# Gate projection by block products between the merge steps of the triangular inverse, with an image trip on two queues and another load order

## The chip, the core and the metric

The kernel runs on one core of one Trainium2 chip. The core has TensorE (PE, matrix products into PSUM), VectorE (DVE), ScalarE (ACT), GpSimd (POOL) and SyncE (SP, which here only issues DMAs), each with an instruction stream of its own; they wait for each other by semaphores. Sixteen DMA engines move data between HBM and SBUF. Everything is float32. The metric is the device time of one execution in microseconds (us), the median of the runs shown.

## The reference

One inference step of a decoder layer: 256 prompt tokens and 8 x 4 sample tokens, 288 columns in all, of width 1024. Cut to what matters here:

```python
h = rmsnorm(x, norm1_w)
proj = h @ w_in          # pool 512, q/k/v 3072, b/a 16, z 1024, gate_pool 1024, gate_delta 1024
...
A = (kb @ k.T) * decay * strict                  # per head and chunk of the sequence
t_inv = triangular_solve(eye + A, eye)           # unit lower triangular inverse
... # scan over chunks with t_inv; for samples: S = S * a + k_dec^T v_new
merged = sigmoid(gate_pool) * branch_pool + sigmoid(gate_delta) * branch_delta
x = x + merged @ w_out
x = x + moe(rmsnorm(x, norm2_w))                 # 32 experts, top 2; all experts' weights are read
```

The 16 column chunks of the two gates (128 columns each, 8 + 8) are the products that the change rewrites. The expert weights are 96 matrices of 1 MB.

## The kernel before

**Stages.** First the projection `proj = h @ w_in`, chunk by chunk of 128 output columns, with convolution, pooling and norms beside it; then the chunked delta rule: a prep per head, the inverse of `eye + A`, a scan; then the two branch products, the output product with the router, and eight quads of four experts each (gate, up, down). All engines follow orders written out by hand, one function per engine.

**Chunks and pairs.** A weight item of w_in is two chunks, 1 MB, in a ring slot of SBUF (`SLOT_OF` says which; slots 0 to 5). `proj(n)` (L1417) makes one chunk with eight products of 128x128 by 128x288, accumulated in PSUM bank n % 2; ScalarE evacuates it (`evac`, L951; tanh for the gates). Items 1 to 11 (`FAST`, the q/k/v chunks) are made another way: `fast_pair` (L1439) takes both chunks of an item as a 2 x 2 block matrix and makes seven block products (four products of 128x128 by 128x144 each) in place of eight. GpSimd forms four sums of weight blocks per pair (`sum_weights`, L754), VectorE had formed four sums of token blocks once, and VectorE and ScalarE add the products.

**Around the inverse.** The gate chunks are 36 to 51. The first nine (`LEAD_GATES`) run ahead of the inverse, the last seven (`LATE_GATES`) between its steps. The inverse needs the 16 x 16 diagonal blocks of A spread over partitions. This goes through DRAM: once all eight heads are prepared (`prep_done`), SP writes the image `a_image` (1 MB), reads eight blocks back (`diagonal_blocks`, L488), VectorE inverts them by forward substitution (15 steps, `sub_done`), SP writes eight blocks to `x_image` and reads it as X (256 KB). Then TensorE, VectorE and ScalarE merge the blocks 16 to 32, 32 to 64, 64 to 128: `inner_y`, `inner_xx`, `middle_y`, `middle_xx`, `outer_y`, `outer_xx` (L1688 to L1742).

**Sample states.** Between the merge steps stand four state units (`state_unit`, L1675: four products of 32x128 by 32x512). Each needs a spread of the new sample values over a tile `vx` (semaphore `vx_done`), and its results are added by VectorE (`state_adds`) to states that GpSimd has scaled after `sub_done`, eight operations of 128x1024 (L854). The first spread serves units 0 and 1, the second units 2 and 3; VectorE makes both (L2652).

**Loads.** SP issues everything in one order (a loop over the items, L560 on): each load waits until the reader of its slot is done. `DIAG_AT` puts the image trip into this order, `STORE_AT` the stores of the states. In the expert stage `gates`, `ups` and `downs` (L604 to L614) load four matrices each into fixed slots, once the products of an earlier quad have read them (`m_gate`, `m_up`, `m_dn1`); `pair_loads` (L647) sets their order.

Of the kernel before, what the change touches and what calls it, by code (L numbers as in the profile page):

```python
# [12 lines left out]
P = 128  # L13
# [8 lines left out]
H = 8  # L22
# [32 lines left out]
FAST = range(1, NQKV // 2)  # L55
SQUARES_AT = (2, 4, 7, 8)
HT, HK = T // 2, KD // 2
P1, P6, P5, P7, P2, P3, P4 = range(1, 8)
SUM2, SUM4, SUM7, SUM5, SUM6 = range(1, 6)
SLOT_OF = [i % 4 if i < NQKV // 2 else i % RA for i in range(A_ITEMS)]  # L60
# [6 lines left out]
def sums_slot(i):  # L67
    return 4 + i % 2


def reader_ahead(i, s):
    users = [j for j in range(i) if SLOT_OF[j] == s or (j in FAST and sums_slot(j) == s)]
    return max(users, default=None)
# [15 lines left out]
LEAD_GATES = 9  # L89
Z_AHEAD = 2  # L90
LATE_GATES = range(N_GATE + LEAD_GATES, N_PROJ)
# [10 lines left out]
STORE_AT = (IN_ITEMS + BP_ITEMS + 1, IN_ITEMS + BP_ITEMS + 3)  # L102
# [3 lines left out]
DIAG_AT = (N_GATE + 2) // 2 + RA - 1  # L106


EVEN_GATES, ODD_GATES = (8, 9, 11, 12), (2, 3, 4, 5)
UPS, DOWNS = (13, 14, 15, 6), (7, 10, 0, 1)  # L110
# [4 lines left out]
SECOND_DOWNS = (EARLY_DOWN,) + DOWNS[1:]  # L115

# [14 lines left out]
def hybrid_step(nc, x_prompt, x_sample, cache_pool, cache_conv, state_delta, norm1_w, w_in, w_pool,  # L131
# [24 lines left out]
    with ExitStack() as ctx:  # L156
# [250 lines left out]
        def item_read(i):  # L407
            if i < IN_ITEMS:
                return S["proj"], product(i, P4) if i in FAST else chunk(2 * i + 1)
# [10 lines left out]
        for n in range(N_PROJ):  # L420
            free[n] = (free[n - 1] if n else 0) + (1 if n // 2 in FAST else 2 if n < N_POOL else 3 if n < N_Z else 1)


        def chunk(n):
            return n + 1 + 5 * sum(1 for i in FAST if i < n // 2)
# [10 lines left out]
        def weights_summed(i, k):  # L436
            return 1 + 4 * FAST.index(i) + k
# [10 lines left out]
        def weight_sums(i):  # L448
            return slots[sums_slot(i)].rearrange("p (j k n) -> p j k n", j=4, k=HK)

# [12 lines left out]
        def delta_sums(j):  # L463
# [11 lines left out]
                      ((108, 109), o_norm_w)]  # L475
        block = ctx.enter_context(nc.Block())
# [3 lines left out]
        def _(sp):  # L480
# [7 lines left out]
            def diagonal_blocks():  # L488
                sp.wait_ge(S["prep_done"], H)
                sp.dma_start(a_image, AT.rearrange("p g i -> p (g i)")).then_inc(S["diag"], 16)  # L490
                sp.wait_ge(S["diag"], 16 * 2)
                for m in range(8):
                    sp.dma_start(And[16 * m:16 * m + 16, :].rearrange("g (j i) -> g j i", i=16),
                                 a_blocks[m].rearrange("j g i -> g j i")).then_inc(S["diag"], 16)
                sp.wait_ge(S["sub_done"], 1)
                for m in range(8):
# [2703 lines left out]
```

## Time and profile before

| | |
|---|---|
| median of 3 runs | 574.17 us (573.9 to 576.23) |
| profiled execution | 574.23 us, span 572.3 us |
| TensorE busy | 534.9 us, 93% of the span |
| VectorE, ScalarE, GpSimd busy | 280.1, 152.8, 138.1 us |
| chunk products (128x288) | 480 records, 122.6 us |
| block products (128x144) of the first stage | 616 records, 78.3 us |
| DMA queue of SP | 153.69 MB, 73.2% of 16 engines' span |

A float32 product stands twice in TensorE's records, so eight products of a chunk are 16 records. The span is the profiled part of the execution. Busy time is an average over stages with different limits; the stage table below tells them apart. A row of a timeline gives start, length, engine, line of the kernel, operation, tiles written and read, and count; in brackets the idle time ahead of it and what ended it.

### The profile page before, as it was taken

Reading aid. Unit: us, or ns where it says so; the run is one execution under the profiler, and the core shown is the slowest. Engines: PE = TensorE matmul, PEld = TensorE weight load, DVE = VectorE, ACT = ScalarE, POOL = GpSimd, SP = SyncE. Lnnn points to the kernel's source line nnn. Section 1 sums busy time; section 2 is a strip of 40 time slices with the busy share of each in tenths; the row PEclk is TensorE's granted clock in tenths of the full one; section 3 lists DMA queues with packets and bytes.
Section 4 is the critical chain, followed back from the end, with each engine's and each line's share of the span. In section 5 each row is a group of like instructions: output and inputs, shape, how many; then the busy total and the mean of one; then the engine's idle time right before and its main releaser. Section 6 shows DMA issues by size and latency. Waiting matters only on the chain. (4 is left out here: it accounts for less than half of the span.)

```text
span 572.3 us, 12784 instructions
## 1 busy us (share of the span) xinstructions
PE 534.9 (93%) x5156; PEld 405.9 (71%) x5156; DVE 280.1 (49%) x811; ACT 152.8 (27%) x408; POOL 138.1 (24%) x226
## 2 busy tenths in 40 slices
PE   7999999999999999999999999999998969599984
PEld 6899999877777776779799788657454535266442
DVE  3867768783543726446756344533523242405135
ACT  3258465315851002133100124210011101010105
POOL 6687677013030090024133222000000000000001
PEclk9999999999999999999999999999997989899988
DMA  9845454657984063853478898899999999999992
GB/s 259 239 124 155 122 161 149 213 174 268 319 253 148 10 219 106 254 155 108 128 259 341 350 424 299 347 396 425 401 421 420 419 420 423 420 419 420 419 361 96
DMA packets 81228, 158.00 MB, mean 276 GB/s; under 512 B 11166, under 2 KB 65067, under 8 KB 68979
## 3 DMA queue, kind: packets, MB, share of 16 engines
q1 hardware_dynamic: 78604, 153.69, 73.2%
q10 hardware_dynamic: 2567, 3.51, 2.1%
q8 instruction: 41, 0.67, 0.5%
q14 instruction: 16, 0.13, 0.1%
HBM read 149.40 MB, written 7.96 MB: 275 GB/s over the span
## 5 line engine op out<-in xcount | busy, mean ns | idle before, releaser
L1428 PE MATMUL ps<-arena 128*128 128x288 f32 x480 | 122.6, 410 | 1.7 <-issue 1.0
L1428 PEld LDWEIGHTS ps<-arena 128*128 128x128 f32 x480 | 89.4, 190 | 27.3 <-issue 3.1
L2092 PE MATMUL ps<-arena 128*32 128x256 f32 x1024 | 65.9, 417 | 15.0 <-DMA arena<-in_w_up_dram 13.4
L1435 PE MATMUL ps<-arena 128*128 128x144 f32 x616 | 78.3, 287 | 0.0
L1435 PEld LDWEIGHTS ps<-arena 128*128 128x128 f32 x616 | 76.3, 190 | 2.4 <-issue 1.9
L2092 PEld LDWEIGHTS ps<-arena 128*32 128x32 f32 x1024 | 38.0, 120 | 41.0 <-issue 25.6
L908 POOL TENSOR_TENSOR arena<-arena 128x512 f32<-128x512 f32 x2 | 2.5, 1276 | 207.2 <-ACT arena L1341 207.2
L2368 DVE SCALAR_TENSOR_TENSOR ps<-arena,ps 128x312 f32<-128x312 f32 x72 | 39.1, 545 | 2.2 <-ACT ps L1028 0.9
L1381 PE MATMUL ps<-arena 128*128 128x128 f32 (+7 forms) x162 | 26.7, 284 | 7.2 <-DVE arena L3069 5.1
L2007 PE MATMUL ps<-arena 128*128 128x128 f32 x256 | 32.3, 279 | 0.8 <-DVE arena L3047 0.7
L2007 PEld LDWEIGHTS ps<-arena 128*128 128x128 f32 x256 | 29.8, 192 | 3.7 <-issue 2.5
L1951 PE MATMUL ps<-arena 128*128 128x256 f32 x128 | 31.0, 385 | 0.0
L1381 PEld LDWEIGHTS ps<-arena 128*128 128x128 f32 (+7 forms) x162 | 18.9, 149 | 14.9 <-issue 6.4
L3069 DVE TENSOR_TENSOR arena<-arena,ps 128x256 f32<-128x256 f32 x8 | 3.4, 421 | 51.2 <-issue 40.8
L1903 PE MATMUL ps<-arena 128*128 128x144 f32 x224 | 27.9, 286 | 0.2 <-DVE arena L2887 0.2
L1903 PEld LDWEIGHTS ps<-arena 128*128 128x128 f32 x224 | 27.6, 190 | 0.6 <-DVE arena L2887 0.5
L2153 PE MATMUL ps<-arena 128*32 128x512 f32 x224 | 25.5, 595 | 0.6 <-ACT arena L1265 0.5
L3085 DVE TENSOR_TENSOR arena<-arena,ps 128x512 f32<-128x512 f32 (+1 forms) x35 | 21.6, 633 | 9.0 <-PE ps L2173 9.0
L1951 PEld LDWEIGHTS ps<-arena 128*128 128x128 f32 x128 | 23.1, 190 | 3.0 <-issue 0.4
L979 ACT ACTIVATE arena<-ps 128x288 f32<-128x288 f32 x16 | 6.6, 411 | 58.9 <-PE ps L1428 58.9
L3018 DVE COPY arena<-ps 128x512 f32<-128x512 f32 x8 | 5.5, 690 | 32.0 <-PE ps L2007 32.0
L3076 DVE COPY sc<-ps 128x512 f32<-128x512 f32 x7 | 4.8, 692 | 32.2 <-PE ps L2153 32.2
(442 smaller groups left out, 802.5 us busy)
## 6 DMA issues: line engine op xcount, KB each, us to landing
arena<-in_w_gate_dram SPq DMA_DIRECT2D x32, 1024.0 KB, 13.2
arena<-in_w_up_dram SPq DMA_DIRECT2D x32, 1024.0 KB, 16.9
arena<-in_w_down_dram SPq DMA_DIRECT2D x28, 1024.0 KB, 17.0
arena<-in_w_in_dram SPq DMA_DIRECT2D x26, 1024.0 KB, 5.8
out_dram<-arena SPq DMA_DIRECT2D x9, 512.0 KB, 7.2
arena<-in_w_branch_delta_dram SPq DMA_DIRECT2D x4, 1024.0 KB, 5.9
arena<-in_w_out_dram SPq DMA_DIRECT2D x4, 1024.0 KB, 5.2
arena<-in_state_delta_dram SPq DMA_DIRECT2D x7, 512.0 KB, 8.6
```

The costliest lines, as they stand in the source:

```text
L979: nc.scalar.activation(gT[:, n - N_GATE, :], src[:, 0:T], ACT.Tanh, scale=0.5).then_inc(S["proj_free"], 1)
L1381: return nc.tensor.transpose(out, in_, ident[0:m, 0:m])
L1428: last = mm(ps[n % 2][:, 0:T], w[:, k, P * (n % 2):P * (n % 2) + P], hT[:, k, :], start=(k == 0), stop=(k == KD - 1))
L1435: last = mm(to[:, 0:HT], left[:, k, :], right[:, k, :], start=(first and k == 0), stop=(k == HK - 1), skip_group_check=True)
L1903: last = mm(bank[:, 0:HT], left[:, k, :], right[:, k, :], start=(first and k == 0), stop=(k == HK - 1), skip_group_check=True)
L1951: last = mm(bank[:, 0:256], merged[:, k, P * t:P * t + P], w[:, k, :], start=(k == 0), stop=(k == KD - 1))
L2007: ins = mm(to, x2p[:, t, k, :], G[:, t, :], start=(first and k % 4 == 0), stop=(last_tile and k % 4 == 3), skip_group_check=True)
L2092: last = mm(to[CAP * e:CAP * e + CAP, 0:FE], xgT[:, k, CAP * e:CAP * e + CAP], w[e][:, k, :], start=(k == 0), stop=(k == KD - 1))
L2153: last = mm(ps[5 + half][CAP * e:CAP * e + CAP, :], actT[:, c, CAP * e:CAP * e + CAP], w[:, c, 512 * half:512 * half + 512], start=(c == 0 ...
L2368: ins = V.scalar_tensor_tensor(c, e[:, j:j + NACC], smallT[:, NQKV * j + n:NQKV * j + n + 1], c, ALU.mult, ALU.add)
L3018: V.tensor_copy(xgT[:, 0:4, :].rearrange("p k t -> p (k t)"), ps[0][:, :]).then_inc(S["m_xg0"], 1)
L3085: V.tensor_tensor(v, v, bank[:, 0:v.shape[1]], ALU.add).then_inc(S["m_yadd"], 1)
```

## The change

Three parts, in one diff.

1. Six early gate chunks stay before (36 to 41, `LEAD_GATES` = 6); the other ten become five pairs of seven block products (`LATE_FAST`, items 21 to 25). They use PSUM banks 0 and 1 alone, the sums of tokens are formed again into slot 0 and a spare strip (`sum_tokens`), and the sums of weights by GpSimd into slots 5 and 1 in turn. The first pair runs whole ahead of `inner_y`, the last whole behind the last state unit; the three between are cut into a piece of four blocks and a piece of three, laid between the merge steps. VectorE's additions and the merge steps are interleaved, a part of `middle_merge` goes to ScalarE, and the second spread (`vx`) goes to GpSimd.
2. The image trip: `a_image` is written in two parts (six heads, then two), and the eight block reads and eight block writes are split over SP's and ScalarE's queues.
3. Slots change (`SLOT_OF`, `ODD_GATES`, `DOWNS`); in the expert stage the third quad's up weights are loaded ahead of the second quad's down weights, and two of the third quad's down weights go to slots that the second quad's up weights leave (`third_downs`).

```diff
-LEAD_GATES = 9
+LEAD_GATES = 6
+LATE_FAST = range(IN_ITEMS - 5, IN_ITEMS)
+LEAD_PAIR, PAIR_A, PAIR_B, PAIR_C, PAIR_D = LATE_FAST
-DIAG_AT = (N_GATE + 2) // 2 + RA - 1
+DIAG_AT = LATE_FAST[1]
-STORE_AT = (IN_ITEMS + BP_ITEMS + 1, IN_ITEMS + BP_ITEMS + 3)
+STORE_AT = (IN_ITEMS + BP_ITEMS - 2, IN_ITEMS + BP_ITEMS - 1)
...
@@ SP @@
             def diagonal_blocks():
+                rows = AT.rearrange("p g i -> p (g i)")
-                sp.wait_ge(S["prep_done"], H)
-                sp.dma_start(a_image, AT.rearrange("p g i -> p (g i)")).then_inc(S["diag"], 16)
+                for heads, cols in ((IMAGE_FIRST // 2, slice(0, IMAGE_FIRST * P)), (H, slice(IMAGE_FIRST * P, 2 * H * P))):
+                    sp.wait_ge(S["prep_done"], heads)
+                    sp.dma_start(a_image[:, cols], rows[:, cols]).then_inc(S["diag"], 16)
...
                 if isinstance(i, int) and i == 0:
+                    ups(2, then)
                     downs(1, first + QE)
-                    ups(2, then)
                     gates(3, then + QE, 1)
+                    third_downs(then)
...
@@ GpSimd @@
             own_columns(1)
+            sum_weights(LATE_FAST[0])
             pool.wait_ge(S["sd_pe"], 2)
             nc.gpsimd.memset(X[:, 2 * H * TILE:6 * H * TILE], 0.0).then_inc(S["memsets"], 1)
             pool.wait_ge(S["sub_done"], 1)
+            sum_weights(LATE_FAST[1])
             for h in range(H):
                 nc.gpsimd.tensor_tensor(state[h], state[h], eGd[:, h, :].unsqueeze(2).to_broadcast([P, BD, P]),
                                         ALU.mult).then_inc(S["sd_mul"], 1)
+            sum_weights(LATE_FAST[2])
+            sum_weights(LATE_FAST[3])
+            pool.wait_ge(S["sdn_pe"], 2)
+            pool.wait_ge(S["decdve"], 8)
+            nc.gpsimd.tensor_tensor(vx, vnq[:, 1, :].unsqueeze(1).to_broadcast([P, BD, P]), spread(bmask4, P, P),
+                                    ALU.mult).then_inc(S["vx_done"], 1)
+            sum_weights(LATE_FAST[4])
...
@@ ScalarE @@
+            act.wait_ge(S["diag"], 16 * IMAGE_WRITES)
+            for m in BY_SCALAR:
+                read_diagonal(act, m)
             for n in range(N_GATE + 3, N_GATE + LEAD_GATES):
+                if n == N_GATE + LEAD_GATES - 1:
+                    act.wait_ge(S["sub_done"], 1)
+                    for m in BY_SCALAR:
+                        write_inverse(act, m)
                 evac(n)
...
@@ TensorE @@
+            def late_products(i):
...
+                late_block(0, a11, lambda k: hT[:, k, 0:HT])
+                pe.wait_ge(S["pads"], weights_summed(i, 2))
+                late_block(1, s2, lambda k: late_summed[1][k])
+                pe.wait_ge(S["proj_free"], late_free(i, 1))
+                late_block(0, s1, lambda k: late_summed[0][k])
+                pe.wait_ge(S["pads"], weights_summed(i, 3))
+                pe.wait_ge(S["sums"], late_added(i, L_SUM2))
+                late_block(1, s3, lambda k: late_summed[2][k])
+            def late_products_back(i):
...
+            late_products(LEAD_PAIR)
+            late_products_back(LEAD_PAIR)
             inner_y()
-            proj(LATE_GATES[0])
+            late_products(PAIR_A)
             inner_xx(0)
             state_unit(0)
             inner_xx(1)
-            proj(LATE_GATES[1])
+            late_products_back(PAIR_A)
             state_unit(1)
             middle_y()
-            proj(LATE_GATES[2])
+            late_products(PAIR_B)
             state_unit(2)
             middle_xx()
-            proj(LATE_GATES[3])
+            late_products_back(PAIR_B)
             outer_y()
-            proj(LATE_GATES[4])
+            late_products(PAIR_C)
             outer_xx()
-            proj(LATE_GATES[5])
+            late_products_back(PAIR_C)
             state_unit(3)
-            proj(LATE_GATES[6])
+            late_products(PAIR_D)
+            late_products_back(PAIR_D)
...
@@ VectorE, after the substitution @@
+            new_values()
+            spread_v()
             sample_output()
+            late_u2(LEAD_PAIR)
+            late_u4(LEAD_PAIR)
+            late_u7(LEAD_PAIR)
+            late_c12(LEAD_PAIR)
+            late_c21(LEAD_PAIR)
+            late_c11(LEAD_PAIR)
```

TensorE's order from the last sample tiles to the third state unit, before (128x288: chunks; 128x512: state units; 32x32: merge products):

```order
L1620 MATMUL ps<-arena 32x128 x8
L1428 MATMUL ps<-arena 128x288 x32
L1694 MATMUL ps<-arena 32x32 x64
L1428 MATMUL ps<-arena 128x288 x8
L1704 MATMUL ps<-arena 32x32 x32
L1684 MATMUL ps<-arena 128x512 x4
L1704 MATMUL ps<-arena 32x32 x32
L1428 MATMUL ps<-arena 128x288 x8
L1684 MATMUL ps<-arena 128x512 x4
L1714 MATMUL ps<-arena 32x32 x32
L1428 MATMUL ps<-arena 128x288 x8
L1684 MATMUL ps<-arena 128x512 x4
```

The same place after (128x144: block products, four to a block):

```order
L1710 MATMUL ps<-arena 32x128 x8
L1845 MATMUL ps<-arena 128x144 x28
L1784 MATMUL ps<-arena 32x32 x64
L1845 MATMUL ps<-arena 128x144 x16
L1794 MATMUL ps<-arena 32x32 x32
L1774 MATMUL ps<-arena 128x512 x4
L1794 MATMUL ps<-arena 32x32 x32
L1845 MATMUL ps<-arena 128x144 x12
L1774 MATMUL ps<-arena 128x512 x4
L1804 MATMUL ps<-arena 32x32 x32
L1845 MATMUL ps<-arena 128x144 x16
L1774 MATMUL ps<-arena 128x512 x4
```

Four chunks ahead of the first merge product became one whole pair, and each chunk between became a piece of a pair; the third state unit (the last row) stands behind the first piece of the third pair.

GpSimd's order from the wait for the substitution to the branch weights' sums, with the semaphores that a row waits for, before (128x1024: scalings of the states; `late_room` holds one of them):

```order
L854 TENSOR_TENSOR arena<-arena,sc 128x1024 [waits sub_done]
L854 TENSOR_TENSOR arena<-arena,sc 128x1024 x3
L854 TENSOR_TENSOR late_room<-late_room,sc 128x1024
L854 TENSOR_TENSOR arena<-arena,sc 128x1024 x3
L867 TENSOR_TENSOR arena<-arena 128x512 [waits ring_in4,merge,y_pe]
```

After, from the last of the four sums that now follow that wait (128x512: sums of weights, four to a pair; the row of L915 is the spread):

```order
L820 TENSOR_TENSOR arena<-arena 128x512 [waits pads]
L909 TENSOR_TENSOR arena<-arena,sc 128x1024 x4
L909 TENSOR_TENSOR late_room<-late_room,sc 128x1024
L909 TENSOR_TENSOR arena<-arena,sc 128x1024 x3
L815 TENSOR_TENSOR arena<-arena 128x512 [waits proj,ring_in2]
L817 TENSOR_TENSOR arena<-arena 128x512 [waits pads]
L818 TENSOR_TENSOR arena<-arena 128x512
L820 TENSOR_TENSOR arena<-arena 128x512 [waits pads]
L815 TENSOR_TENSOR arena<-arena 128x512 [waits proj,ring_in3]
L817 TENSOR_TENSOR arena<-arena 128x512 [waits pads]
L818 TENSOR_TENSOR arena<-arena 128x512
L820 TENSOR_TENSOR arena<-arena 128x512 [waits pads]
L915 TENSOR_TENSOR arena<-arena 128x1024 [waits decdve,sdn_pe]
```

Ahead of the scalings stand four sums, behind them eight, and then the second spread.

SP's loads for the second and third quad, before (up, down and gate weights; `m_gate`, `m_up`, `m_dn1` count the products that have read a slot):

```order
L601 DMA arena<-in_w_gate_dram 128x2048 x3
L601 DMA arena<-in_w_down_dram 128x2048 [waits m_dn1]
L601 DMA arena<-in_w_down_dram 128x2048 x2
L601 DMA arena<-in_w_up_dram 128x2048 [waits m_up]
L601 DMA arena<-in_w_up_dram 128x2048 x3
L601 DMA arena<-in_w_gate_dram 128x2048 [waits m_gate]
```

After:

```order
L643 DMA arena<-in_w_up_dram 128x2048 [waits m_up]
L643 DMA arena<-in_w_up_dram 128x2048 x3
L643 DMA arena<-in_w_down_dram 128x2048 [waits m_dn1]
L643 DMA arena<-in_w_down_dram 128x2048 x2
L643 DMA arena<-in_w_gate_dram 128x2048 [waits m_gate]
L643 DMA arena<-in_w_gate_dram 128x2048 x3
L643 DMA arena<-in_w_down_dram 128x2048 [waits m_up]
L643 DMA arena<-in_w_down_dram 128x2048
L643 DMA arena<-in_w_down_dram 128x2048 [waits m_dn1]
```

The four up loads moved ahead of the three down loads, and the third quad's four down loads are cut in two, with a wait each.

## Rows read from the trace of the kernel before

**Rows 1.** Stage table: stretch, length, busy (count) by engine, clock, DMA share, GB/s.
```profile
180.00:251.00 71.00, 69.66 (x830) 51.03 (x829) 32.49 (x72) 9.27 (x20) 20.83 (x13) 1.00 0.49 152
...
367.00:548.00 181.00, 160.03 (x1948) 91.87 (x1939) 61.70 (x172) 17.53 (x38) 0.00 (x0) 0.95 1.01 415
```

**Rows 2.** TensorE's timeline (start, length): gate chunks, merge products, state units.
```profile
193.21 15.79 PE L1428 MATMUL ps<-arena 128*128 128x288 f32 x64
208.93 1.29 PE L1694 MATMUL ps<-arena 32*32 32x32 f32 x128
...
215.49 0.75 PE L1704 MATMUL ps<-arena 32*32 32x32 f32 x64
...
218.48 4.15 PE L1428 MATMUL ps<-arena 128*128 128x288 f32 x16
222.56 1.14 PE L1684 MATMUL ps<-arena 32*128 32x512 f32 x8
...
224.76 4.15 PE L1428 MATMUL ps<-arena 128*128 128x288 f32 x16
228.84 1.14 PE L1684 MATMUL ps<-arena 32*128 32x512 f32 x8
...
250.49 1.04 PE L1381 MATMUL ps<-arena 128*128 128x128 f32 x8
```

**Rows 3.** TensorE's timeline: one pair of seven block products in the first stage.
```profile
70.35 7.03 PE L1435 MATMUL ps<-arena 128*128 128x144 f32 x56
77.21 0.27 PE L1381 MATMUL ps<-arena 128*118 128x128 f32 x1
```

**Rows 4.** SP queue's timeline: image written, blocks read, inverse read.
```profile
179.78 0.34 SPq L490 DMA_DIRECT2D a_image<-arena  x1
185.16 4.05 SPq L493 DMA_DIRECT2D arena<-a_image  x8
...
205.17 0.35 SPq L502 DMA_DIRECT2D arena<-x_image  x1
```

**Rows 5.** VectorE's timeline: substitution's first and last operation, the flip behind X.
```profile
190.70 0.29 DVE L2695 TENSOR_SCALAR arena<-arena 128x256 f32<-128x256 f32 x1 [0.31 <-DMA arena<-a_image]
...
199.75 0.39 DVE L2702 TENSOR_REDUCE arena<-arena 128x15 f32<-128x225 f32 x1
...
207.95 0.71 DVE L2714 STREAM_TRANSPOSE arena<-arena 128x512 f32<-128x512 f32 x1 [5.79 <-DMA arena<-x_image]
```

**Rows 6.** GpSimd's timeline: scalings of the states, four sums of weights.
```profile
200.21 7.47 POOL L854 TENSOR_TENSOR arena<-arena,sc 128x1024 f32<-128x1024 f32 x4 [15.21 <-DVE arena L2702]
...
209.50 5.60 POOL L854 TENSOR_TENSOR arena<-arena,sc 128x1024 f32<-128x1024 f32 x3
242.30 1.27 POOL L867 TENSOR_TENSOR arena<-arena 128x512 f32<-128x512 f32 x1 [27.20 <-DVE arena L2733]
...
246.10 1.27 POOL L872 TENSOR_TENSOR arena<-arena 128x512 f32<-128x512 f32 x1
```

**Rows 7.** VectorE's timeline: operations beside a sum of GpSimd, and without one.
```profile
294.60 0.30 DVE L2917 TENSOR_TENSOR arena<-arena,ps 128x144 f32<-128x144 f32 x1
294.93 1.28 DVE L2891 SCALAR_TENSOR_TENSOR arena<-arena 128x288 f32<-128x288 f32 x1
...
308.65 0.46 DVE L2891 SCALAR_TENSOR_TENSOR arena<-arena 128x288 f32<-128x288 f32 x1
```

**Rows 8.** Stage table: a wait of TensorE in the expert stage, and behind it.
```profile
492.22:498.65 6.43, 0.00 (x0) 0.03 (x1) 0.66 (x3) 0.38 (x1) 0.00 (x0) 0.74 1.00 417
498.65:502.10 3.45, 3.45 (x36) 1.87 (x40) 0.00 (x0) 0.00 (x0) 0.00 (x0) 0.50 1.02 425
```

**Rows 9.** Stage table: the start of the expert stream.
```profile
374.00:384.00 10.00, 9.40 (x116) 6.59 (x108) 2.07 (x3) 1.03 (x3) 0.00 (x0) 1.00 1.00 386
384.00:402.00 18.00, 17.40 (x258) 11.20 (x261) 7.36 (x22) 1.67 (x4) 0.00 (x0) 1.00 1.01 423
402.00:410.00 8.00, 8.00 (x72) 3.05 (x68) 4.87 (x11) 0.60 (x1) 0.00 (x0) 1.00 0.98 386
```

## The prediction made before the change was run

> **What bounds the kernel now.** I read the stage table first, because one kernel can have several limits. Between 180 and 251 us TensorE is busy 69.66 of 71.00 us while the DMA engines move 152 GB/s: a TensorE stage. From 367 to 548 us the DMA engines stand at 1.01 and TensorE works 160.03 of 181 us: the expert weights arrive no faster than 415 GB/s, and TensorE waits for them [rows 1]. What is saved ahead of 367 us therefore comes through in full only because it lets this stream start earlier. Behind 367 us only idle time of the DMA engines can be saved.
>
> Next I read TensorE's own order of time in the stage that the change rewrites [rows 2]. The reader is to see that it has almost no gap: the four last early gate chunks at 193.21, the inner product of the triangular inverse at 208.93, then gate chunks laid between the merge steps, to the first head transposes at 250.49. The merge chain runs on VectorE and ScalarE beside the chunks, and a chunk covers each of its steps. So the question is what stands late once the chunks are shorter. For that I read VectorE, GpSimd and the SP queue over the same stretch [rows 4 to 6].
>
> **Part 1, the gate products.** Ten chunks (eight products of 288 columns each) become five pairs of seven blocks (four products of 144 columns per block). Four chunks in a row take 15.72 us, from 193.21 to 208.93, so 3.93 each; a chunk that stands alone takes 4.08, from 224.76 to 228.84 [rows 2]. A pair of the first stage takes 6.86 us, from 70.35 to 77.21, so 0.98 a block [rows 3]. Two chunks in a row, 7.86, against 6.86: 1.0 us a pair, 5.0 us for five. A piece that stands alone pays an opening, as the lone chunk does: 4.08 - 3.93 = 0.15 us; eight pieces stand in place of one run and seven chunks, so that this is even. The saving of 5.0 us holds if nothing else is late. The thirty additions on VectorE, 0.30 us each [rows 7], and the ten copies on ScalarE lie beside the block that runs meanwhile, 0.98 long; without that cover they would cost 30 x 0.30 = 9 us.
>
> **Part 2, who is late next.** The weights' four sums for each pair are new work on GpSimd, and the second spread of the sample values moves from VectorE to GpSimd, behind the sums of the fourth pair. TensorE waits for that spread before the third state unit, and everything after it (the middle merge, three more pieces, the scan) is queued behind that wait. So I follow GpSimd from the point where it is released, the end of the forward substitution.
>
> Before, the image is written at 179.78 and its first block is read back at 185.16 [rows 4]; the substitution starts at 190.70 and ends at 199.75 + 0.39 = 200.14, so it lasts 9.44 us and starts 5.54 us after the first read's issue [rows 5]. After, only 256 KB are left to write once the last head is prepared. The nearest row is the 256 KB read of the other image, issued at 205.17 and used at 207.95: 2.78 us [rows 4, 5]. That puts the first read at 182.56. The eight reads took 4.05 us to issue, 0.51 each; with four on each of two queues, 2.03 us of this goes. The substitution starts at 182.56 + 5.54 - 2.03 = 186.1 and ends at 195.5. The Trainium skill (Trainium Kernel Development and Optimization, section Key Constraints) says that queues of several engines share the same 16 DMA engines and that issuing from several saves the issue time alone; by that rule, too, only the 2.03 us go, and the image trip gets no shorter through a second queue in any other way. Bounds for the end of the substitution: 195.0, if the small write lands 0.5 us sooner than the read did, and 200.1, if the two queues and the split bring nothing.
>
> From there GpSimd does, in order, with no wait between that would let it go earlier:
> - four sums for the second pair: 242.30 to 246.10 + 1.27 = 5.07 us [rows 6];
> - a collision with VectorE's first spread, now at the same time, which reads two operands from SBUF. Such an operation of VectorE took 1.28 us beside a sum of GpSimd and 0.46 us alone [rows 7], so one of the two stands while the other runs; I put 1.0 us on GpSimd (0 to 1.3, one sum's length);
> - eight scalings of the states: 200.21 to 209.50 + 5.60 = 14.89 us [rows 6];
> - the sums of two more pairs: 10.14 us;
> - the spread itself, 1024 elements as a scaling: 7.47 / 4 = 1.87 us [rows 6].
>
> Together 33.0 us, so 195.5 + 33.0 = 228.5 (226.7 to 233.4). Before, the third state unit starts at 228.84 [rows 2]. The unit thus starts 0.3 us earlier than now, and no more, however short the products ahead of it.
>
> TensorE is there long before. The third early chunk and the sample tiles, now the other way round, end at 193.21 + 3.93 = 197.1. Then: first pair 6.9, wait for one gate's copy 0.5, inner product 1.3, four blocks 4.1, inner merge and first unit 218.48 - 215.49 = 3.0, three blocks 3.1, second unit and middle product 224.76 - 222.56 = 2.2, four blocks 4.1: about 222.3 [rows 2, 3]. It waits some 6.2 us, and the 5 us saved lie in that wait.
>
> **Part 3, behind that wait.** Four chunks become pieces of 3, 4, 3 and 7 blocks, 17 in all: 17 x 0.98 + 4 x 0.15 = 17.3 us, against four chunks of 4.08, 16.3: 1.0 us more, because 17 of 28 blocks that remain after the first pair, the work of 4.9 chunks, now stand behind the wait. VectorE's four state additions stand ahead of the last pair's first sum, so I take 1.2 us (0.8 to 1.6). The stage of 21.65 us from 228.84 to 250.49 then ends at 228.5 + 21.65 + 1.2 = 251.35, 0.9 us later than before.
>
> **Part 4, the clock.** After a wait of TensorE of 6.43 us in the stream the granted clock stood at 0.50 for the next 3.45 us [rows 8]: 1.2 in place of 2.4 GHz, so half of these, 1.7 us, are lost. I take 1.7 (0 to 2.5). The rows show this in the expert stage alone. The Trainium skill (TensorE: Matmul & The Clock Gate, part 1) makes it a rule for any idle stretch, that an idle array goes back to half rate and has to earn the full one; by it the 1.7 us are due here too, and without it the sum below is 1.7 us lower, which is a rival below.
>
> **Part 5, the loads of the third quad.** The stream dips twice: 386 GB/s in 374 to 384 and in 402 to 410, against 423 between them [rows 9]; 10 x 37 / 423 + 8 x 37 / 423 = 0.9 + 0.7 = 1.6 us. The up weights, free earlier, now stand ahead of the down weights of the second quad, and two of the third quad's down weights go into slots that are free before the second quad ends, so the queue should hold work at both places. I take 1.2 us back (0 to 1.6). The down weights of the second quad land later, but the stream needs some 10 us for the four matrices put ahead of them and TensorE still has two products and a gather in front of them.
>
> The rest I cost at nothing. VectorE's five sums of tokens end before the image's blocks can be there at 186.1; were they in the way, some 3 us (by 0.46 us for 288 elements) would come on top of the substitution. The last loads on SP (four branch matrices, now behind all stores of the states) are issued some 15 us later, but the products that read them follow the scan, which starts at 250.49; if they were late, TensorE would wait there and the stream's start with it. Two DMA issues of ScalarE's queue stand ahead of one gate's copy: the 0.5 us above.
>
> **Sum.** Against the profiled execution, 574.23 us (span 572.3 and 1.9 around it; the median of the runs is 574.17): +0.9 + 1.7 - 1.2 = +1.4, and 0.3 us for some ten semaphore passes in the GpSimd chain: 575.9 us.
>
> **Rivals.**
> - The saving arrives: GpSimd isn't what TensorE waits for, the third unit starts at 222.3, without clock loss. Then 222.3 + 21.65 + 1.2 = 245.15, 5.3 us earlier, less 1.2: 567.7 us. For it speaks that GpSimd was idle from 215.1 to 242.3, room enough for its 20 us of new sums. Against it: those sums stand ahead of and behind the scalings in one queue, and GpSimd would need 6.2 us less for 33 us whose pieces all have a row. Together with cases that go half this way, 0.10.
> - Slower: the image round trip isn't shorter (the second part waits on the queue, or the writes on ScalarE's queue land late). Each us that the substitution ends after 195.5 is added in full. With 200.1 the result is 575.9 + 4.6 = 580.5; from 196.7 on it is slower by over 0.5%. 0.17.
> - The clock stays up: 574.2 us. 0.20.
> - The stream gets nothing back, since its engines are at 0.98 to 1.00 in the dips as well: 577.1 us. 0.13.
> - The forecast, 575.9, with 574.0 to 577.8 as its own range: 0.40.
>
> **Numbers.** 0.5% is 2.87 us, about what a measurement of this kernel can tell from no change: below 571.3 is faster, above 577.0 slower. Faster: 0.10. Slower: 0.17, half of the fourth rival and 0.08 of the forecast's upper end, 0.31. Within: 0.59. The range leaves out most of the first case and the far end of the second: 572.3 to 579.5.
>
> **What the profile would show.** Right: the third state unit (four products of 512 columns, after the third pair's first piece) at 228 to 229.5 after a wait of TensorE of 5 us or more, released by GpSimd, whose new spread ends just ahead of it; the substitution's end at 195 to 196; the granted clock at 0.5 behind the wait; the head transposes at 252 to 254; no dip of the stream between 374 and 410 plus the shift. Wrong: TensorE dense through that place and the transposes ahead of 248, or a wait before another step (a block product behind VectorE's additions), or a stream that starts on time and still ends later.

## The result: 580.51 us, one per cent slower

The changed kernel takes 580.51 us (median of 8 runs, 578.62 to 583.51), the kernel before 574.76 us beside it; the ratio is 1.0096, 95% interval 1.0078 to 1.0115. A second series of the same kernel gave 579.93 us and 1.0113 (1.0079 to 1.0147). The forecast, 575.9, put the loss at a third of this, and the range ended at 579.5. One rival of the prediction names this very time, 580.5, but for an image trip that is no shorter; the trace shows one that ends 3.8 us earlier, so that the agreement is chance.

**One correction first.** Two profiled executions are compared by a place that the change doesn't touch. GpSimd clears a tile once the state products are made; this is where that starts, in the kernel before and then in the changed one (start, length, engine, line):

```profile
184.05 0.95 POOL L851 MEMSET arena<- 128x1024 f32 x1 [18.09 <-PE ps L1632]
```

```profile
183.01 0.95 POOL L905 MEMSET arena<- 128x1024 f32 x1 [11.96 <-PE ps L1722]
```

TensorE's order up to here is the same in both. GpSimd's first four sums, VectorE's sums of tokens and the first part of the image already lie ahead of it in the changed kernel, but they don't make the lead: the 1.04 us are there at the first chunk of the projection, which starts at 12.28 us, against 13.32 in the kernel before. Over all kernels below this place lies between 183.01 and 186.19. So I compare lengths from one place to the next, not times since the start. The profiled execution's span grew by 577.7 - 572.3 = 5.4 us; counted from here it is 6.4.

TensorE's timeline of the changed kernel, the places of [rows 2]: first merge product, third pair's first piece, third state unit, three blocks behind it, outer merge, last pair, head transposes, first branch product:

```profile
204.23 1.29 PE L1784 MATMUL ps<-arena 32*32 32x32 f32 x128
...
217.64 4.38 PE L1845 MATMUL ps<-arena 128*128 128x144 f32 x32
228.15 2.09 PE L1774 MATMUL ps<-arena 32*128 32x512 f32 x8 [6.12 <-POOL arena L915]
...
232.02 5.89 PE L1845 MATMUL ps<-arena 128*128 128x144 f32 x24
237.84 1.15 PE L1829 MATMUL ps<-arena 64*64 64x64 f32 x32
...
248.32 7.14 PE L1845 MATMUL ps<-arena 128*128 128x144 f32 x56
255.30 1.04 PE L1471 MATMUL ps<-arena 128*128 128x128 f32 x8
...
292.67 1.14 PE L2040 MATMUL ps<-arena 128*128 128x144 f32 x8
```

The reader is to see the wait of 6.12 us ahead of the third state unit, released by GpSimd's spread (L915), and what stands behind it: the unit takes 2.09 us where it took 1.14 [rows 2], and three blocks take 5.89 us, 1.96 each, where the four ahead of the wait take 4.38. The stage table of the changed kernel gives the clock (stretch, length, busy time and count of PE, PEld, DVE, ACT, POOL, granted clock, DMA share, GB/s):

```profile
180.00:251.00 71.00, 64.19 (x907) 54.10 (x905) 39.32 (x98) 11.33 (x25) 38.41 (x26) 0.93 0.38 107
222.03:228.15 6.12, 0.00 (x1) 0.00 (x1) 0.30 (x1) 0.00 (x0) 5.99 (x5) 0.93 0.00 0
227.29:237.53 10.24, 9.38 (x127) 7.81 (x128) 3.77 (x7) 1.62 (x3) 0.81 (x1) 0.50 0.01 2
237.53:255.30 17.77, 17.77 (x188) 16.44 (x188) 7.42 (x18) 3.54 (x8) 4.99 (x4) 1.00 0.96 290
379.70:389.70 10.00, 9.40 (x116) 6.58 (x108) 2.07 (x3) 1.05 (x3) 0.00 (x0) 1.00 1.01 419
407.70:415.70 8.00, 8.00 (x72) 3.04 (x68) 4.85 (x11) 0.60 (x1) 0.00 (x0) 1.00 1.01 421
```

The second row is the wait: TensorE idle, GpSimd busy for 5.99 of 6.12 us. In the third the clock stands at 0.50, the lower of its two levels (1.2 of 2.4 GHz), for 10.24 us, and TensorE works through 9.38 of them. The last two rows are the places of the stream's dips [rows 9], shifted by 5.7 us: no dip is left.

Who TensorE waits for, on VectorE (substitution's first and last operation, first spread):

```profile
185.88 0.29 DVE L2874 TENSOR_SCALAR arena<-arena 128x256 f32<-128x256 f32 x1 [1.64 <-DMA arena<-a_image]
...
194.93 0.39 DVE L2881 TENSOR_REDUCE arena<-arena 128x15 f32<-128x225 f32 x1
...
195.68 2.06 DVE L2831 TENSOR_TENSOR arena<-arena 128x1024 f32<-128x1024 f32 x1
```

and on GpSimd (sums of weights 128x512, scalings, the spread, sums of the branch weights):

```profile
195.40 1.27 POOL L815 TENSOR_TENSOR arena<-arena 128x512 f32<-128x512 f32 x1 [11.43 <-DVE arena L2881]
196.74 2.14 POOL L817 TENSOR_TENSOR arena<-arena 128x512 f32<-128x512 f32 x1
...
201.29 7.48 POOL L909 TENSOR_TENSOR arena<-arena,sc 128x1024 f32<-128x1024 f32 x4
...
216.14 1.27 POOL L815 TENSOR_TENSOR arena<-arena 128x512 f32<-128x512 f32 x1
...
226.19 1.90 POOL L915 TENSOR_TENSOR arena<-arena 128x1024 f32<-128x1024 f32 x1
...
265.44 1.27 POOL L929 TENSOR_TENSOR arena<-arena 128x512 f32<-128x512 f32 x1 [22.32 <-DMA arena<-in_w_branch_delta_dram]
```

From the substitution's end, 195.32, to the third state unit, 228.15, it is 32.83 us; GpSimd stands still nowhere between. The ledger gives each length from one place to the next. The first branch product of the kernel before:

```profile
286.96 1.14 PE L1903 MATMUL ps<-arena 128*128 128x144 f32 x8
```

| from, to | before | after | difference |
|---|---|---|---|
| end of state products, third state unit | 44.79 | 45.14 | +0.35 |
| third state unit, head transposes | 21.65 | 27.15 | +5.50 |
| head transposes, first branch product | 36.47 | 37.37 | +0.90 |
| first branch product, end of span | 285.34 | 285.03 | -0.31 |

### The profile page after: what moved, and what is told of

Read it like the earlier page. It is cut to its first block and busy times, and to the rows that moved or that the text cites. A ratio compares the mean times of both kernels' runs of the same rounds, so it can differ in the third digit from the quotient of the medians.

```text
span 577.7 us, 13128 instructions
## 1 busy us (share of the span) xinstructions
PE 532.1 (92%) x5276; PEld 411.5 (71%) x5276; DVE 292.9 (51%) x843; ACT 155.5 (27%) x415; POOL 166.2 (29%) x247
## 5 line engine op out<-in xcount | busy, mean ns | idle before, releaser
L1518 PE MATMUL ps<-arena 128*128 128x288 f32 x320 | 81.4, 409 | 0.7 <-DVE arena L2482 0.7
L1525 PE MATMUL ps<-arena 128*128 128x144 f32 x616 | 78.3, 287 | 0.0
L1525 PEld LDWEIGHTS ps<-arena 128*128 128x128 f32 x616 | 76.3, 190 | 2.4 <-issue 1.9
L2231 PE MATMUL ps<-arena 128*32 128x256 f32 x1024 | 63.0, 403 | 14.7 <-DMA arena<-in_w_up_dram 12.9
L1518 PEld LDWEIGHTS ps<-arena 128*128 128x128 f32 x320 | 59.7, 190 | 17.2 <-issue 1.7
L2231 PEld LDWEIGHTS ps<-arena 128*32 128x32 f32 x1024 | 35.7, 116 | 40.1 <-issue 23.0
L970 POOL TENSOR_TENSOR arena<-arena 128x512 f32<-128x512 f32 x2 | 2.5, 1274 | 206.5 <-ACT arena L1431 206.5
L1845 PE MATMUL ps<-arena 128*128 128x144 f32 x280 | 39.9, 303 | 0.4 <-issue 0.2
L1845 PEld LDWEIGHTS ps<-arena 128*128 128x128 f32 x280 | 37.6, 202 | 2.3 <-issue 1.4
L2144 PEld LDWEIGHTS ps<-arena 128*128 128x128 f32 x256 | 29.8, 192 | 3.6 <-issue 2.5
L2040 PE MATMUL ps<-arena 128*128 128x144 f32 x224 | 27.9, 286 | 0.2 <-DVE arena L3100 0.2
L2040 PEld LDWEIGHTS ps<-arena 128*128 128x128 f32 x224 | 27.6, 190 | 0.6 <-DVE arena L3100 0.4
L815 POOL TENSOR_TENSOR arena<-arena 128x512 f32<-128x512 f32 x16 | 20.3, 1271 | 24.0 <-DVE arena L2881 11.4
L2088 PEld LDWEIGHTS ps<-arena 128*128 128x128 f32 x128 | 23.1, 190 | 3.0 <-issue 0.4
```

The costliest lines, as they stand in the source:

```text
L815: nc.gpsimd.tensor_tensor(s1, a21, a22, ALU.add).then_inc(S["pads"], 1)
L1518: last = mm(ps[n % 2][:, 0:T], w[:, k, P * (n % 2):P * (n % 2) + P], hT[:, k, :], start=(k == 0), stop=(k == KD - 1))
L1525: last = mm(to[:, 0:HT], left[:, k, :], right[:, k, :], start=(first and k == 0), stop=(k == HK - 1), skip_group_check=True)
L1845: last = mm(ps[bank][:, 0:HT], left[:, k, :], right(k), start=(opens and k == 0), stop=(k == HK - 1), skip_group_check=True)
L2040: last = mm(bank[:, 0:HT], left[:, k, :], right[:, k, :], start=(first and k == 0), stop=(k == HK - 1), skip_group_check=True)
L2088: last = mm(bank[:, 0:256], merged[:, k, P * t:P * t + P], w[:, k, :], start=(k == 0), stop=(k == KD - 1))
```

## The experiments

The kernel before took 574.67 us beside the first four experiments and 574.40 beside the others. My theory after the result: the wait behind GpSimd's queue, and the low clock behind the wait, are the loss; the scan loses 0.9 us to GpSimd's sums that now run beside it. The rivals: the pieces are slow for a reason of their own, or what is saved at the wait is taken back by the next one.

**The wait taken away at its source.** The spread moves ahead of four sums in GpSimd's queue:

```diff
             sum_weights(LATE_FAST[2])
-            sum_weights(LATE_FAST[3])
             pool.wait_ge(S["sdn_pe"], 2)
             pool.wait_ge(S["decdve"], 8)
             nc.gpsimd.tensor_tensor(vx, vnq[:, 1, :].unsqueeze(1).to_broadcast([P, BD, P]), spread(bmask4, P, P),
                                     ALU.mult).then_inc(S["vx_done"], 1)
+            sum_weights(LATE_FAST[3])
```

> GpSimd makes the second spread ahead of the four sums for the fourth pair, not behind them. Theory (the wait of 6.12 us behind GpSimd's chain and the low clock behind it are the whole loss): four sums of 1.27 us, 5.07 us, leave the chain, so the third state unit starts at 223.1 in place of 228.15, TensorE waits about 1.1 us in place of 6.12, the granted clock stays at 1.00 there, and the 4.7 us that 9.4 us at half rate cost are not lost: first head transposes at 255.3 - 5.05 - 4.7 = 245.6, the run 9.7 us shorter than the changed kernel, about 570.8 us. Rival (the saving meets the next wait): the fourth pair's sums, now 223.1 to 228.2, or the last pair's come too late, TensorE waits there, and at most 5 us come through: 575 us or more. Second rival (the low clock has nothing to do with the wait): only the 5 us of the wait go and the clock falls all the same: 575.5 us.

Measured: 571.31 us, ratio to the kernel before 0.9951 (0.9932 to 0.9971), 9.2 us less than the changed kernel. TensorE's timeline of this kernel:

```profile
225.70 1.14 PE L1774 MATMUL ps<-arena 32*128 32x512 f32 x8 [0.67 <-POOL arena L914]
...
248.53 1.04 PE L1471 MATMUL ps<-arena 128*128 128x128 f32 x8
```

and its stage table from the unit to the transposes:

```profile
225.70:248.53 22.83, 22.83 (x313) 20.70 (x313) 11.11 (x25) 5.16 (x11) 9.88 (x8) 1.00 0.75 227
```

The wait is 0.67 us, the clock stays at 1.00, and unit to transposes is 22.83 us. Neither rival holds. Against 21.65 before, 22.83 is 1.18 us more: the price of what now stands behind the unit, 17 blocks in place of four chunks.

**The wait kept, TensorE kept busy in it.** Six block products more, into a bank that nobody reads:

```diff
             late_products(PAIR_B)
+            for _ in range(6):
+                for k in range(HK):
+                    mm(ps[4][:, 0:HT], late_left(PAIR_B)[0][:, k, :], hT[:, k, 0:HT], start=(k == 0), stop=(k == HK - 1))
             state_unit(2)
```

> TensorE makes six block products more (24 products of 144 columns, into a PSUM bank that nobody reads before it is written again) ahead of the third state unit; they add about 5.9 us of work, which ends at 227.9, within the wait of 6.12 us. The wait's end stays where it is, 228.15. Theory (the low clock of 10.24 us follows from TensorE's idle time): the clock stays at 1.00, the transposes come at 255.3 - 4.7 = 250.6, and the run takes 4.7 us less than the changed kernel, about 575.8 us. Rival (the products behind the wait are slow for another reason, or the clock's loss is only the 1.7 us that the prediction put): the gain is 1.7 us or less, 578.8 us or more; if the clock falls in spite of the filling, 580.5 us.

Measured: 577.68 us, ratio 1.0052 (1.0031 to 1.0073), 2.8 us less than the changed kernel. The filling, and the stage table from the unit to the transposes:

```profile
225.58 6.04 PE L1899 MATMUL ps<-arena 128*128 128x144 f32 x48
231.56 1.14 PE L1774 MATMUL ps<-arena 32*128 32x512 f32 x8
```

```profile
231.56:254.39 22.83, 22.83 (x313) 20.70 (x313) 11.11 (x25) 5.15 (x11) 5.00 (x4) 1.00 0.75 227
```

The clock stays at 1.00 and the same work takes 22.83 us, to the hundredth what it takes without a wait. So 27.15 - 22.83 = 4.32 us are the clock's, and they come from TensorE's idleness, not from the pieces. In the trace 4.4 us are gone from the state products to the end, 3.4 against the repeated run of the changed kernel; the medians show 2.8 of the 4.7 that I expected. So the clock's cost is read from the traces at this place; the medians show its direction and not its size.

**Shorter waits.** The spread between the second and the third sum of the fourth pair (its three statements, unchanged, become `second_spread`):

```diff
                 nc.gpsimd.tensor_tensor(s2, s1, a11, ALU.subtract).then_inc(S["pads"], 1)
+                if amid:
+                    amid()
...
-            sum_weights(LATE_FAST[3])
+            sum_weights(LATE_FAST[3], second_spread)
```

> GpSimd makes the second spread between the second and the third of the four sums for the fourth pair. The third state unit starts two sums, 2.5 us, earlier than in the changed kernel and TensorE waits some 3.6 us there. Theory (the wait and the low clock behind it, whose length is not proportional to the wait: behind a wait of 3.56 us the granted clock stood at 0.50 for 6.83 us in the kernel with the image trip on one queue, behind 6.12 us for 10.24): 2.5 us of wait and 4.7 - 3.4 = 1.3 us of clock come back, 576.7 us. Rival (a wait of this length costs no clock): 2.5 + 4.7 = 7.2 us come back, 573.3 us. Second rival (any such wait costs the whole 10.24 us at half rate): 578.0 us.

Measured: 577.57 us, 1.0049 (1.0029 to 1.0068). The first rival, 573.3, is refuted. The time alone doesn't tell the theory's 576.7 from the second rival's 578.0; the trace below does, with a low stretch of 6.82 us and not 10.24. And VectorE makes the spread, which GpSimd leaves out:

```diff
                 state_adds(1, range(3, 4))
+                dve.wait_ge(S["sdn_pe"], 2)
+                V.tensor_tensor(vx, vnq[:, 1, :].unsqueeze(1).to_broadcast([P, BD, P]), spread(bmask4, P, P),
+                                ALU.mult).then_inc(S["vx_done"], 1)
                 late_u7(PAIR_B)
```

> VectorE makes the second spread again, as before, behind the state additions of the second unit and ahead of one addition of the third pair; the rest is the changed kernel. Theory (the spread is late only because it stands behind sums in GpSimd's queue): the spread runs from about 221.7 to 224, the third state unit starts at about 224 after a wait of 2 us, 0.9 us behind the kernel with the spread ahead of the sums: 572.2 us if the clock stays up, 575.6 us if it falls for 6.83 us. Rival (VectorE is the wrong place too, since its operation and GpSimd's sums hold each other up): third unit at 226 or later, 577 us or more.

Measured: 572.25 us, 0.9966 (0.9944 to 0.9987). Third unit and low clock of the first kernel, then of the second:

```profile
227.86 1.31 PE L1778 MATMUL ps<-arena 32*128 32x512 f32 x8 [3.40 <-POOL arena L917]
```

```profile
228.71:235.53 6.82, 6.82 (x119) 6.37 (x116) 3.77 (x7) 1.18 (x2) 1.55 (x2) 0.50 0.01 2
```

```profile
225.84 1.14 PE L1770 MATMUL ps<-arena 32*128 32x512 f32 x8 [1.56 <-DVE arena L2927]
```

```profile
227.45:230.86 3.41, 3.41 (x73) 3.35 (x64) 2.27 (x5) 1.18 (x2) 1.92 (x2) 0.50 0.02 5
```

So a spread on VectorE comes within 1 us of one that stands ahead in GpSimd's queue: it was not the move to GpSimd that cost the time, but its place there. The clock fell here too, for 3.41 us. The time meets the forecast for a clock that stays up, 572.2; that the clock fell in the profiled execution, the slowest of the ten (575.45 us), makes this agreement partly luck.

**The image trip of before, inside the changed kernel.**

```diff
-IMAGE_FIRST = 12
-BY_SYNC, BY_SCALAR = range(4), range(4, 8)
-IMAGE_WRITES = 3
+BY_SYNC, BY_SCALAR = range(8), ()
+IMAGE_WRITES = 2
```

> The image trip of the kernel before inside the changed kernel: the image written in one piece after the last head, all eight reads and eight writes on SP's queue. Theory (the end of the substitution sets GpSimd's chain, and this the third state unit): the substitution ends at about 199.9 in place of 195.32, the third state unit starts 4.6 us later at 232.7, the run takes 4.6 us more, about 585.1 us. Rival (the trip is hidden: GpSimd's chain is tied to something else): 580.5 us. A wait of some 3.7 us ahead of the first merge product, where the inverse's read now lands later, comes out of the later wait and adds nothing by itself.

Measured: 581.52 us, 1.0121 (1.0093 to 1.0149), 1.0 to 1.6 us more than the changed kernel, not 4.6; the intervals of the two overlap. The third unit:

```profile
232.90 1.18 PE L1773 MATMUL ps<-arena 32*128 32x512 f32 x8 [3.56 <-POOL arena L914]
```

The substitution ends at 200.07, and to the unit it is again 32.83 us: the chain is as I said. But counted from the state products the substitution ends only 15.34 - 12.31 = 3.03 us later, and the wait is only 3.56 us, since TensorE comes to it later: it stood 3.20 us ahead of the sample tiles, and the clock was at 0.50 there from 199.74 to 206.57. That low stretch adds nothing by itself, as TensorE would have waited at the third unit anyway. Behind the shorter wait the clock costs 3.08 us in place of 4.32: 3.03 - 1.24 = 1.8 us more at the transposes.

**The load order of before.**

```diff
-                    ups(2, then)
                     downs(1, first + QE)
+                    ups(2, then)
                     gates(3, then + QE, 1)
```

> In the changed kernel the second quad's down weights are loaded ahead of the third quad's up weights again, as before; the rest of the load order stays. Theory (the reordering gave the stream back the 1.4 us by which its lag behind the kernel before shrinks between 370 and 410 us): the two dips of the stream come back and the run takes 1.4 us more, about 581.9 us. Rival (a dip is filled here and another opens later, the end of the stream being set elsewhere): within 0.5 us of 580.5 us.

Measured: 580.61 us, 1.0103 (1.0053 to 1.0152): no difference to be told. The stage table at the place of the first dip and of the second:

```profile
380.90:390.90 10.00, 9.40 (x116) 6.60 (x108) 2.07 (x3) 1.03 (x3) 0.00 (x0) 1.00 1.00 397
...
408.90:416.90 8.00, 8.00 (x72) 3.06 (x68) 4.87 (x11) 0.60 (x1) 0.00 (x0) 1.00 1.00 419
```

Only the first dip returns, and in part: 10 x (419 - 397) / 421 = 0.5 us. The second stays filled without the new order. What this edit left there are the third quad's down weights in their new slots; that these fill it follows by elimination and wasn't tried alone.

**The first branch matrix loaded earlier**, on top of the first experiment (slots 1 and 4 change places, in the tables of the expert stage too; one store moves):

```diff
-SLOT_OF = [i % 4 if i < NQKV // 2 else i % RA for i in range(LATE_FAST[0])] + [3, 4, 2, 3, 4, 2, 3, 4, 0, 1, 5, 2, 3, 4, 0]
+SLOT_OF = [i % 4 if i < NQKV // 2 else i % RA for i in range(LATE_FAST[0])] + [3, 4, 2, 3, 4, 2, 3, 1, 0, 4, 5, 2, 3, 1, 0]
-STORE_AT = (IN_ITEMS + BP_ITEMS - 2, IN_ITEMS + BP_ITEMS - 1)
+STORE_AT = (IN_ITEMS + BP_ITEMS - 2, IN_ITEMS + BP_ITEMS)
```

> On top of the kernel with the spread ahead of the fourth pair's sums (571.3 us): the first branch matrix is loaded into the slot that comes free at the end of the fourth pair (slots 1 and 4 change places) and ahead of the second half of the states' stores. Theory (the 0.9 us that the changed kernel loses in the scan come from GpSimd's four sums of that matrix, which now run beside the scan, and from VectorE's small operations standing behind them): the sums run some 8 us earlier, beside the last gate pair, VectorE's operation on 128x4 elements takes 0.3 us and not 1.3, and the way from the first head transposes to the first branch product gets 0.9 us shorter: about 570.4 us. Rival (the scan waits for something else of the change, the additions of the last pair say): same time, 571.3 us.

Measured: 571.60 us, 0.9948 (0.9926 to 0.9970): in the time no gain over 571.31 shows. In the trace the way from the transposes (248.15) to the first branch product (284.84) is 36.69 us, against 37.37 in the first experiment and 36.47 before: 0.7 of the 0.9 us. The operation that stood behind a sum, in the kernel before, in the changed one (with the sum beside it) and here:

```profile
264.58 0.29 DVE L2801 TENSOR_SCALAR sc<-sc 128x4 f32<-128x4 f32 x1
```

```profile
269.25 1.26 POOL L934 TENSOR_TENSOR arena<-arena 128x512 f32<-128x512 f32 x1
```

```profile
269.39 1.29 DVE L3014 TENSOR_SCALAR sc<-sc 128x4 f32<-128x4 f32 x1
```

```profile
262.24 0.52 DVE L3014 TENSOR_SCALAR sc<-sc 128x4 f32<-128x4 f32 x1
```

Here it takes 0.52. I expected 0.3; another set of GpSimd's sums still stands beside it. The other traces bear the cause out: over all ten this operation takes between 0.29 and 1.41 us (0.87 where the wait is filled, with a way of 36.95), and the way from the transposes to the first branch product, less the operation's own length, is always 36.06 to 36.18 us.

**The changed kernel again**, in one series with the spread between the sums, the spread on VectorE and the earlier branch matrix:

> The changed kernel once more, on the same chip and in the same stretch of time as the three others, so that differences of one or two us are read against it: 580.5 us, with the third state unit behind a wait of some 6 us and the clock at 0.50 for 10.24 us. If its time lies a few tenths of a per cent off, the profiled execution's lead of 1.0 us over the kernel before at an untouched place (the end of the state products) is chance.

Measured: 579.93 us; a wait of 5.83 us, the clock at 0.50 for 10.24 us. The lead of 1.04 us was chance: here the same place lies at 184.62. Its ledger: 45.23, 26.77, 37.40 and 284.28 us.

The waits ahead of the third unit, side by side, in us (the cost is the way from the unit to the transposes, less 22.83):

| kernel | wait | clock at 0.50 for | unit to transposes | cost of the clock |
|---|---|---|---|---|
| wait filled | 0 | - | 22.83 | 0 |
| spread ahead | 0.67 | - | 22.83 | 0 |
| spread ahead, matrix earlier | 1.10 | - | 22.83 | 0 |
| spread on VectorE | 1.56 | 3.41 | 24.35 | 1.52 |
| spread between sums | 3.40 | 6.83 | 25.91 | 3.08 |
| image on one queue | 3.56 | 6.83 | 25.91 | 3.08 |
| changed, again | 5.83 | 10.24 | 26.77 | 3.94 |
| old load order | 5.84 | 10.24 | 26.91 | 4.08 |
| changed | 6.12 | 10.24 | 27.15 | 4.32 |

## Why the prediction was wrong, step by step

- **Part 2, who is late:** right. TensorE waits 6.12 us (forecast 6.2) at the step named, released by the spread named; GpSimd's chain is 32.83 us (33.0), its collision with VectorE's spread 2.14 - 1.27 = 0.87 us (1.0). The saved time lies in the wait.
- **The image trip:** the right mechanism, a little too large. From the state products the substitution ends 3.8 us earlier than before, not 4.6. The reads start 181.09 - 178.74 = 2.35 us after the write (2.78 forecast), but the substitution starts 4.79 us after the first read, not 3.51. With the chain this makes the third unit 0.35 us later, not 0.3 earlier. The times since the start, 195.32 for the substitution's end and 228.15 for the unit, lie in the ranges that the prediction named, the first by luck: without the lead of 1.04 us it is 196.36. (The lower bound of the unit should read 195.0 + 32.0 = 227.0, not 226.7; nothing rests on it.)
- **Part 3, the pieces behind the wait:** right, 1.18 us for 1.2. How the 1.18 divide between the blocks and VectorE's additions wasn't measured.
- **Part 4, the clock: the step that failed.** I took 1.7 us (0 to 2.5) from the 3.45 us that the clock stood at 0.50 behind a wait of 6.43 us [rows 8]. That row is cut off by where I began it. The stage table of the kernel before, cut where the clock changes:

```profile
492.22:495.27 3.05, 0.00 (x0) 0.00 (x0) 0.66 (x3) 0.38 (x1) 0.00 (x0) 1.00 1.01 419
495.27:502.10 6.83, 3.45 (x36) 1.90 (x40) 0.00 (x0) 0.00 (x0) 0.00 (x0) 0.50 1.01 420
```

The low stretch was 6.83 us long there, and half of it lay inside the wait, where it costs nothing. Ahead of the third state unit it began at 227.29, 0.86 us before the wait ended, lasted 10.24 us, and cost 4.32 us, above my upper bound. One row had shown one case, and I took its case for the bound. The Trainium skill (TensorE: Matmul & The Clock Gate, part 1) says that an idle array goes back to half rate and has to earn the full one; the traces agree, with 0.50 behind each of the waits of 1.56 us and more ahead of the third unit. The prediction read it as a rule for any idle stretch; waits of 0.67 and 1.10 us at the same place left the clock at 1.00. The rival in which the clock stays up is refuted.
- **The scan: a term that was missing.** I wrote that the products that read the branch matrices follow the scan, so that the later loads cost nothing. GpSimd's sums of the first of them don't follow it: they ran at 242.30 [rows 6], ahead of the scan, and now at 265.44, inside it, where VectorE stands behind them. +0.90 us in the trace. The loads came far later than the "some 15 us" of the prediction; SP's issues of the four matrices, two to a row before, all in one row after:

```profile
215.59 13.71 SPq L568 DMA_DIRECT2D arena<-in_w_branch_delta_dram  x2
...
240.38 10.68 SPq L568 DMA_DIRECT2D arena<-in_w_branch_delta_dram  x2
```

```profile
255.49 9.96 SPq L610 DMA_DIRECT2D arena<-in_w_branch_delta_dram  x4
```

The first is issued 39.9 us later. The Trainium skill (SBUF — State Buffer, section SBUF: two separate sides) calls the port pair that VectorE and GpSimd share an exclusive lock; an operation on four elements a partition that takes 1.29 us, the length of a sum, fits that.
- **Part 5, the stream:** the dips are filled, 10 x (419 - 386) / 421 + 8 x (421 - 386) / 421 = 1.5 us against 1.2. I put it down to the order of the loads and the new slots together; the order is worth 0.5 of it. That the 1.5 us come through isn't shown: of them only 0.3 are left at the end of the span, in the repeated run 1.1, and over the nine traces with the change this last stretch takes 284.28 to 286.14 us, with the 285.34 of the kernel before among them. What takes the rest between 416 us and the end wasn't traced.

The sum of the forecast, with what was measured: chain +0.35 (-0.3), pieces +1.18 (+1.2), clock +4.32 (+1.7), scan +0.90 (0), rest -0.31 (-1.2, and +0.3 for semaphores): +6.4 in place of +1.7. With the repeated run it is +0.44, +1.18, +3.94, +0.93 and -1.06, together +5.4: the clock is the largest miss either way (2.6 or 2.2 us), ahead of the scan (0.9) and the chain (0.7).

## What to carry to other kernels

A wait of TensorE can cost more than its length: add what the low clock takes from the work behind it, count the low stretch from where the clock falls to where it rises, and take the bound from several waits, not from one. When work is moved onto an engine's queue, ask not only whether the engine has time, but what stands ahead of the one result that somebody waits for: the same spread, four sums earlier, turned a loss of 5.75 us into a gain of 3.4. When a load moves, follow not only the products that read it but every helper that prepares it, and what that helper runs beside.

## What was not expected of the hardware

- The clock fell behind waits as short as 1.56 us, and after the wait had ended: at 227.45 with TensorE at work since 225.84, at 228.71 with work since 227.86. Behind 0.67 and 1.10 us it didn't fall. Its low stretches at this place were 3.41, 6.83 and 10.24 us long, the longer the wait, the longer. That order is no rule: in the expert stage a wait of 4.70 us (spread between sums, work again at 502.00) had a low stretch of 3.41 us and one of 4.73 us (image on one queue, 478.36) one of 6.83, and behind 1.73 us (changed kernel, 559.81) the clock stayed at 1.00.
- Two queues halved the issue of the eight reads (4.05 us before, 1.99 on the longer of the two queues) but not the way to the data: the substitution started 4.79 us after the first read in place of 5.54. Issuing took 2.06 us less; from the end of the issue to the start of the substitution it took 1.3 us more. Why wasn't traced.
- A place that TensorE reaches by the same work in all kernels lies up to 3 us earlier or later from one profiled execution to the next (183.01 to 186.19 us over the ten kernels' traces; 183.01 and 184.62 for the changed kernel itself).
